# Output projection by column halves, last solve level as corner tiles, one weight quarter moved into a freed room, and expert matrices in two-megabyte transfers

## What is computed

```python
def reference(x, ...):
    h = layer_norm(x, ln_in_g, ln_in_b)
    mix = hybrid_mixer(h, ...)
    h = layer_norm(alpha * h + mix, ln_mix_g, ln_mix_b)
    ffn = moe_ffn(h, router_w, router_b, moe_w1, moe_w3, moe_w2)
    return layer_norm(alpha * h + ffn, ln_ffn_g, ln_ffn_b)

def hybrid_mixer(h, ...):
    proj = h @ w_in
    y_dn, y_pool, y_ml = ...             # gated DeltaNet, pooling, mLSTM: 512 wide each
    branches = jnp.stack([y_dn, y_pool, y_ml], axis=2)
    y = jnp.einsum('bsrm,rmd->bsrd', branches, w_branch)
    gate = jax.nn.sigmoid(gate_pre.reshape(nb, ns, N_BRANCH, D_MODEL))
    merged = jnp.sum(gate * y, axis=2)
    return merged @ w_out

def gated_delta_rule(q, k, v, beta, g):  # both directions, 4 heads
    ...
    a_mat = m + jnp.eye(CHUNK)           # unit lower triangular
    sol = lax.linalg.triangular_solve(a_mat, rhs, ...)

def expert_block(xblk, e):               # 32 experts, two per token
    act = jax.nn.silu(xblk @ w1[e]) * (xblk @ w3[e])
    return act @ w2[e]
```

## Time and profile before

| | |
|---|---|
| time, median of 3 runs (lowest to highest) | 1263.77 us (1263.27 to 1265.01) |
| the profiled execution's own time | 1264.04 us |
| span of its trace | 1262.2 us |
| PE busy | 1114.3 us (88%) |
| DVE busy | 783.3 us (62%) |
| ACT busy | 599.4 us (47%) |
| POOL busy | 230.8 us (18%) |
| moved by DMA | 284.77 MB, mean 226 GB/s |
| TensorE clock granted, mean | 0.968 of full speed |

### The profile page before, as it was taken

The page is one execution under the profiler, slowest core; times in us unless marked ns, Lnnn a source line. Parts: engine busy times, 40 slices in busy tenths (PEclk is TensorE's granted clock), DMA queues, the critical chain, the costliest instruction groups (busy, mean ns, idle before and its releaser), DMA issues.

```text
span 1262.2 us, 15935 instructions
## 1 busy us (share of the span) xinstructions
PE 1114.3 (88%) x6178; PEld 796.7 (63%) x6178; DVE 783.3 (62%) x1001; ACT 599.4 (47%) x783; POOL 230.8 (18%) x178
## 2 busy tenths in 40 slices
PE   5999998989999999989899499998888888888864
PEld 4788866776767677767478456665555555555532
DVE  6688762575353544534564688876666667776656
ACT  7353436555424333223221366765556555666633
POOL 1000170013322313220000101222222222222100
PEclk9999999999999999999999589999999999999997
DMA  7323421135122212311843699999999999999971
GB/s 255 101 67 100 152 82 34 34 112 184 48 76 67 68 43 68 84 43 59 287 188 143 260 403 401 406 400 402 406 408 407 405 405 406 405 406 415 409 317 69
DMA packets 98178, 284.77 MB, mean 226 GB/s; under 512 B 8904, under 2 KB 58696, under 8 KB 72880
## 3 DMA queue, kind: packets, MB, share of 16 engines
q1 hardware_dynamic: 92992, 274.94, 57.4%
q0 software_dynamic: 4960, 8.22, 2.0%
q10 hardware_dynamic: 144, 0.52, 0.1%
HBM read 269.13 MB, written 22.56 MB: 231 GB/s over the span
## 4 chain that ended last, share of the span: by engine, by line
PE 33%; DMA 29%; DVE 9%; ACT 4%; issue 2%; SPq 1%; POOLq 0%; DVEq 0%; ACTq 0%
DMA wraw<-in_moe_w 27%; PE fill_ps L1251 10%; PE fill_ps L1260 4%; DVE wlo L1987 3%; PE yb L1894 2%; PE hb L2128 2%; ACT whi L1929 2%; PE hb L1866 2%; PE hb L1867 2%; PE lv L1311 1%; PE lv L1321 1%; DMA wraw<-y_dram 1%; PE yb L2128 1%; DMA wraw<-kept_dram 1%; PE lv L1328 1%
## 5 line engine op out<-in xcount | busy, mean ns | idle before, releaser
L1987 DVE TENSOR_TENSOR wlo<-wraw,whi 128x2048 fp32r<-128x2048 f32 x127 | 287.1, 2285 | 129.4 <-ACT whi L1929 129.3
L1929 ACT ACTIVATE whi<-wraw 128x2048 fp32r<-128x2048 f32 x128 | 241.3, 1909 | 152.0 <-DMA wraw<-in_moe_w 137.1
L1866 PE MATMUL hb<-whi,xs 128*128 128x512 f32 x512 | 214.2, 418 | 32.3 <-DVE wlo L1987 30.6
L1867 PE MATMUL hb<-wlo,xs 128*128 128x512 f32 x512 | 202.8, 396 | 0.0
L1251 PE MATMUL fill_ps<-h_part,gws 128*128 128x512 f32 x576 | 159.2, 417 | 0.2 <-DVE gws L1477 0.2
L1894 PE MATMUL yb<-wraw,act_t 128*64 128x512 f32 x512 | 127.5, 626 | 33.0 <-DMA wraw<-in_moe_w 27.2
L1866 PEld LDWEIGHTS hb<-whi,xs 128*128 128x128 f32 x512 | 97.6, 191 | 89.4 <-DVE wlo L1987 46.4
L370 PE MATMUL pj<-h_part,wsplit 128*128 128x512 f32 x528 | 126.0, 397 | 0.0
L1251 PEld LDWEIGHTS fill_ps<-h_part,gws 128*128 128x128 f32 x576 | 104.6, 191 | 27.3 <-issue 5.5
L370 PEld LDWEIGHTS pj<-h_part,wsplit 128*128 128x128 f32 x528 | 99.0, 188 | 24.7 <-issue 3.6
L1867 PEld LDWEIGHTS hb<-wlo,xs 128*128 128x128 f32 x512 | 97.5, 190 | 17.6
(11 more groups left out here) (416 smaller groups left out, 1714.8 us busy)
## 6 DMA issues: line engine op xcount, KB each, us to landing
wraw<-in_moe_w SPq DMA_DIRECT2D x192, 1024.0 KB, 27.4
h<-in_w_in SPq DMA_DIRECT2D x24, 512.0 KB, 4.7
kTok<-in_w_in SPq DMA_DIRECT2D x6, 1024.0 KB, 5.6
vTok<-in_w_in SPq DMA_DIRECT2D x6, 1024.0 KB, 5.6
h<-in_w_in SPq DMA_DIRECT2D x4, 1024.0 KB, 5.6
h<-in_w_branch SPq DMA_DIRECT2D x16, 256.0 KB, 3.0
y_dram<-state SPq DMA_DIRECT2D x8, 512.0 KB, 6.8
kept_dram<-h SPq DMA_DIRECT2D x16, 256.0 KB, 2.2
```

The lines of the kernel that those rows point to most:

```text
L1866: pe.matmul(bank[:, :], lhs, whi[:, u % NSPLIT, cols], start=(half == 0 and kk == 0), stop=False)
L1867: last = pe.matmul(bank[:, :], lhs, wlo[:, u % NSPLIT, cols], start=False, stop=(half == 1 and kk == 3))
L1929: act.activation(whi[:, u % NSPLIT, :], raw[:, room, :], ACT.Copy).then_inc(S.hi_done.sem, 1)
L1987: dve.tensor_tensor(wlo[:, u % NSPLIT, :], raw[:, room, :], whi[:, u % NSPLIT, :].bitcast(F32), ALU.subtract).then_inc(S.lo_done.sem, 1)
```

## The change

Five things are changed.

1. *Corner tiles.* At the last level of the solve (block 64) a direction's products touch one corner of the matrix alone. Now only this corner is multiplied: 64 rows x 64 columns of weights, 4 heads x 2 directions, for both batches of the pair together at the place of b; ACT's copy and DVE's subtraction take 64 rows in place of 128.
2. *Branch quarter.* The fourth row block of `w_branch[0]` goes to the room of the keys (kTok) during `deltanet`, after the last state update has read them, and the load at the start of `back` is gone.
3. *Column halves.* The projection makes half 0 for all four t, then half 1 for all four; turns and logits lie in the second. DVE leaves the second half of w_out's split until the merged groups are done, and takes the statistics of half 0 early. On SP's queue the second half of w_out comes after the last merged group.
4. *Room pairs.* A matrix comes in one transfer of 2 MB into two neighbouring rooms, with one semaphore per pair; it is issued when both halves of the matrix that had the pair are used. Each partition's run in memory is 16 KB in place of 8 KB.
5. *First weights.* Pair 0 comes early as before; pairs 2 and 8 when half 0 is projected; 4, 6 and 10 when all is projected. Nothing of the first twelve rooms waits for the gather any more; the ring does.

```diff
+        def side_rows(side):
+            return slice(64 * side, 64 * side + 64)
...
                     sp.dma_start(v["h2"][:, k, :], w_branch[0][k * P:(k + 1) * P, :]).then_inc(next_bw, 16)
+                sp.wait_ge(ds_done, NB - 2)
+                sp.dma_start(kTok[:, 0:2, :, :].rearrange(...), w_branch[0][(NH - 1) * P:NH * P, :]).then_inc(next_bw, 16)
                 keep(sp, KT - 1)
...
+                        if l < NL - 1:
...
+                        elif d == 1:
+                            for h in range(NH):
+                                for n in (m - 1, m):
+                                    d_, j = BATCH[n][0], at_level(n, l) % 2
+                                    last = pe.matmul(packed(lv[d_][side_rows(1 - d_), :], 0, l)[:, h], ot[side_rows(d_), j, h, side_rows(1 - d_)],
+                                                     halves(tn[side_rows(d_), n % 4, :, :], l, d_)[:, h], start=True, stop=True)
+                                    if h == NH - 1:
+                                        last.then_inc(y1_done, 1)
...
+        def pair_room(q):
+            return raw[:, q % NRAW:q % NRAW + 2, :].rearrange("p a n -> p (a n)")
...
-                if q < begun:
+                if q < begun or half == 1:
                     continue
                 if q >= NRAW:
-                    before, eb, hb_ = units[q - NRAW]
+                    before, eb, _ = units[q - NRAW]
                     if before == "w2":
-                        wait(sp, S.w2_used, 2 * eb + hb_ + 1)
+                        wait(sp, S.w2_used, 2 * eb + 2)
                     else:
-                        wait(sp, S.lo_done, split_unit(eb, before, hb_) + 1)
-                sp.dma_start(raw[:, q % NRAW, :], expert(sp, dram[which], e)[:, half * HALF:(half + 1) * HALF])\
-                    .then_inc(S.w_in[q % NRAW].sem, 16)
+                        wait(sp, S.lo_done, split_unit(eb, before, 1) + 1)
+                sp.dma_start(pair_room(q), expert(sp, dram[which], e)).then_inc(S.w_in[q % NRAW // 2].sem, 16)
...
-                sp.dma_start(h2[:, NH - 1, :], v["w_branch"][0][(NH - 1) * P:NH * P, :]).then_inc(v["next_bw"], 16)
...
-                    if c not in (1, 5):
+                    if c not in (1, KT - 1):
...
-                first_weights(sp, range(2))
+                first_weights(sp, (0,))
                 sp.wait_ge(branch_done, KT)
                 for t in range(NT):
                     sp.dma_start(h2[:, t, :], v["h_dram"][t * P:(t + 1) * P, :]).then_inc(h_in[t], 16)
...
+                sp.wait_ge(out_done, NT)
+                first_weights(sp, (2, 8))
+                for t in range(NT - 1):
+                    sp.wait_ge(h2_ready, t + 1)
+                    sp.dma_start(v["h2_dram"][t * P:(t + 1) * P, :], h2[:, t, :]).then_inc(h2_out, 16)
+                sp.wait_ge(out_done, 2 * NT)
+                first_weights(sp, (4, 6, 10))
+                wait(sp, S.gathered[0], 16)
...
                 for t in range(NT):
                     project(t, 0)
+                for t in range(NT):
+                    project(t, 1, range(4))
                     if t >= 1:
                         turn(t - 1)
...
                     if t >= 2:
                         logits(t - 2)
-                    if t < NT - 1:
-                        project(t, 1)
-                    else:
-                        project(t, 1, range(4))
+                    project(t, 1, range(4, 6))
+                    if t == NT - 1:
                         logits(t - 1)
-                        project(t, 1, range(4, KT))
+                    project(t, 1, range(6, KT))
...
                     if c >= 1:
                         merged_rest(c - 1)
+                    if 1 <= c <= 4:
                         weight_rest(c - 1)
                 merged_rest(KT - 1)
-                weight_rest(KT - 1)
+                for c in range(4, KT):
+                    weight_rest(c)
```

99 lines of the change are left out of this document (55 added, 44 removed).

## The result

The changed kernel takes 1254.07 us (median of 4 runs, 1252.78 to 1255.97) against 1264.39 (1263.27 to 1265.30): a ratio of 0.9921, 95% interval 0.9907 to 0.9936, so 8 to 12 us faster. Forecast were 1249 and 15.

A forecast was written before the change was run, and what follows sets the result against it. PE was taken to bound up to the projection, then the expert weight stream, closely followed by PE. Terms 3.2 + 4.0 + 4.4 + 3.0 = 14.6 us off 1264.0 gave 1249.4, said as 1249; range 1240 to 1258.

The forecast's parts named there:

- Corner tiles: Last solve level: eight y1 and p2 stretches halved, 4.3 us, less two lost to waits: 3.2 us, ends 0 and 4.3.
- 16 KB runs: Expert weight stream: runs of 16 KB in place of 8 KB gain 3.0 us, ends -7 and +7.
- the line: Run time from 2 KB and 8 KB rows, carried on to 16 KB: 605.6 ns, 433 GB/s, worth 7.0 us; under half taken.
- Quarter and halves: Merge and projection: waits for branch weights and DVE go, 4.0 us gained, between 2.5 and 4.6.
- Four units ahead: Ring start: twelve units in instead of eight, worth 11.0 us, less stops for full rooms: 4.4 us, between 0 and 11.0.
- Pairs: Expert stream: a matrix's first half usable 2.75 us later, hidden in flight and at the end; price 0, at most 2.75.
- A: The forecast itself, for the whole kernel: 1245 to 1254 us, chance 0.52.
- C: PE paces first experts; early units, longer runs bring nothing: 1257; sign: unchanged 488 us, ring start to last expert; chance 0.18.
- B: Expert stream never stops, so early units and longer runs count in full: 25.2 us gained, 1239; chance 0.12.
- E: Ring of pairs runs dry in every expert, pairs being held too long: slower, 1272 with 0.8 us per expert; chance 0.06.
- F: Last solve level: products with 64 rows run at half the pace, tiles gain 0: 1252.6; chance 0.04.
- D: Gathers and stores wait behind longer weight pieces, last store 14.4 instead of 7.2 us: 1254; chance 0.08.

The follow-up runs named there:

- e2: The kernel before with the branch quarter and column halves alone, first weights and ring as before: 1258.90 us, ratio 0.9966.
- e5: The changed kernel with the pair of rooms 10 and 11 asked for behind the gather instead of ahead of it: 1252.63 us, ratio 0.9911.
- e3: The changed kernel with each pair loaded by two 1 MB transfers (8 KB runs), rooms and waits of pairs kept: 1257.25 us, ratio 0.9953.
- e4: The changed kernel with the old ring of one-unit transfers, rooms and semaphores, twelve units still asked for ahead: 1258.10 us, ratio 0.9949.

## Why the prediction was right or wrong

The direction and the range (1240 to 1258) were right; the gain of 14.6 was too large by some 4. Of the parts the halves came as forecast; the tiles were mis-sized most, two costs put at nothing were not nothing, and the order of the parts was another: 16 KB runs and halves first, then the early units, tiles last. That the time came out as near as it did is in part luck: 16 KB runs brought more than the share of the line that was taken for want of a row, and 1.0 of the 11.1 us between the profiles lies in stages that weren't changed.

- *Corner tiles, 3.2 forecast, 0.6 measured.* This is the largest miss. The size of one stretch was near (0.47, not 0.54). The step that failed is "I take off two of the eight stretches" for waits. Read against each other, the rows above show where it went: the products behind the wait for ACT stand 3.16 us earlier (562.25 and 559.09), of which the front is 1.01, so 2.15 of the 3.8 were left and 1.6 had been swallowed by waits for DVE; the first branch product stands 1.64 earlier (604.33 and 602.69), so 1.5 more went behind the 2.15 us wait, where PE had the lower clock to 565.8 from the first product on, and before only from 563.3 to 566.7. I had read that PE is 96% busy, and not where the other 4% lie: behind the very steps that were shortened. That fills cover ACT and DVE held for most of the list, but not there.
- *Quarter and halves, 4.0 forecast, 4.0 (e2) to 4.5 measured* (3.1 to 4.5 over all profiles with it). No wait for w_branch, no hole at the projection; the last residual came at 683.6 (forecast 682.5, with the tiles' 3.2).
- *Four units ahead, 4.4 forecast, 2.5 to 3.6 measured.* The gap at the second transfer is where it was foretold and about as long (4.4 us of 712 to 720, forecast 4.6). What the sum lacks is that two of the four bring nothing: with ten ahead (e5) the 30th matrix and the ring's end come as early as with twelve.
- *16 KB runs, 3.0 forecast, 4.4 measured*, within the ends of -7 and +7. The line had 605.6 ns for a run of 16 KB; in the trace it is 614 (and 313 for 8 KB, where the line had 307.7), so the line itself was near. Stretches "at 430 GB/s or above" are few: the rate from 823 to 1203 is 408, before 407.
- *Pairs, 0 forecast, 2.3 lost (one profile each).* I had costed the later first half as hidden in flight and at the end. By the profiles of e3 and e4 it isn't, though their times don't show it. At the end the result rows are used 2.5 us behind the last landing of weights, before 2.4, so the loads did stay in line; but the queue runs emptier there (DMA share, loads of results included, 0.53 and 0.46 in the halves of 1200 to 1210, before 0.60 and 0.99 in those of 1211 to 1221), which the sum had not looked at. The first wait of ACT, said to come later against the ring's start, is no sign of anything here: it came at the same distance (110.5 us, before 110.7) and, in the second profile of the same kernel, an expert later.

```profile
842.47 1.91 ACT L1957 ACTIVATE whi<-wraw 128x2048 fp32r<-128x2048 f32 x1 [5.35 <-DMA wraw<-in_moe_w]
```

- *Routing to gather, nothing forecast, 1.5 lost.* "23 us lie between the residual and the gather's landing" compared the 6 MB with the wrong deadline: the store that the gather waits for comes in the middle of it, and took 3.7 us longer.
- *The end, 0 forecast, 0.3 gained.*

Of the rivals, A's upper end is what came (1254.07, a shade beyond it). C was wrong in its main point (the ring gave 5.4 us, and its 1257 is 3 above the time), but not in all: up to the 30th matrix something other than the kind of transfer sets the pace, and two early units bring nothing. Its sign did come: from the ring's first request to the last expert's first unit 487.7 us, before 488.4. The sign was badly chosen, since both of its ends moved: the ring's first request now follows the gather's landing at once, before it stood 2.0 us behind it, and the last mark now waits for both halves, a unit (2.75 us) later. B: the stream does stop. E: the DMA share beyond 823 is 1.00, no expert runs dry. F: a product of a tile takes 0.22 us, as the old ones did, and they overlap as before (16 records in 0.68 us, 32 in 1.15); they are hidden, not slow. D's time, 1254, is the one that came, but by chance, since D was right in sign alone: gathers land after 10.9 us in place of 9.2 and stores after 8.5 in place of 7.2, and with 8 KB runs again (e3) after 9.1 and 7.0; nothing near the doubling that would have been felt. The Trainium skill (DMA: Bandwidth & Descriptors, section Queues, rings and completion order) states that a DMA engine drains a whole packet of one queue before it switches to another. The direction agrees with this rule; but the runs of the weights doubled (313 to 614 ns) and the landings grew by 18%, so a wait for one such run is at most a part of a landing, and no run here shows how much.

## What to carry to other kernels

Before a step on a nearly full engine is shortened, read which wait comes next behind it on that engine: here steps that ended in a wait for another engine gave nothing or little, and behind one such wait the lower clock lasted longer. Give the freed time work from elsewhere in the same edit, and check that the hole is filled and not moved; here moved fill products were worth more than the tiles in the solves (4.7 us against 0.6). When a queue is filled ahead of a dependent chain, look at each transfer of that chain, stores too, and not only at its end. To judge transfers ahead of a ring of rooms, follow when the n-th one lands: an early gain can be gone before the stretch that counts.

## What the hardware showed

- The first two stages are the same code in all kernels and took from 270.1 to 276.5 us to the first gram product (273.0 before, where "about 280" was said). In the shortest the granted clock was 1.00 from 180 to 270; in the longest 0.89 from 180 to 210 and 0.94 from there to 270. This is as wide as the spread of the runs, so profiles of single executions are compared by stretch.
- A wait of the same 2.15 us was followed by 1.05 us of products in the two profiles without tiles (before, e2), and by 1.6 to 1.9 in all nine with tiles and old fills. Why the lower clock comes earlier and lasts longer there is not shown. Behind the 2.04 us wait the clock fell in two profiles of nine with tiles and such fills (0.83 from 350 to 360), and the solves then took 332.2 in place of 330.7.
- A 2 MB transfer asked for when no other weights were in flight landed after 7.7 to 8.7 us, where 1.3 us to the first bytes and 4.9 at 426 GB/s (both from the rows of before) make 6.2.
- In every kernel with 2 MB transfers the gathers landed after 10.7 to 10.9 us and the stores of results after 8.5 to 8.6 (medians); in every one with 1 MB transfers after 9.0 to 9.2 and 7.0 to 7.2.
